# RG-LRU gate matmuls on 64-row halves of the array, both gates in one operand, and ScalarE evicting 64-partition halves

## The chip, the cores and the metric

The kernel runs on one NeuronCore of a Trainium2 chip. The metric is device time in microseconds (us) for one execution; the comparison is between medians of several runs. TensorE (PE) does the matmuls, ScalarE (ACT) the activations and most of the copies out of PSUM, VectorE (DVE) the elementwise work, GpSimd (POOL) some more of it, and SyncE (SP) issues the DMAs. Each engine runs its own instructions in program order, and semaphores order the engines against each other.

## The reference

One layer of a hybrid decoder: a pre-norm with adaLN shift and scale, one input projection split into two head groups (RG-LRU and HGRN2), one output projection, a post-norm and a residual. It is run over a prompt of 2048 tokens and over 8 decode sequences of 4 tokens. The change concerns the two gates of the RG-LRU, which are block-diagonal: 512 channels are 8 blocks of 64, and each gate multiplies a block by its own 64x64 matrix.

```python
def _rglru(x, h0, wa, ba, wx, bx, lam):
    B, L, _ = x.shape
    xb = x.reshape(B, L, N_BLK_A, BLK_A)                 # 8 blocks of 64 channels
    r = jax.nn.sigmoid(jnp.einsum('blnc,ncd->blnd', xb, wa).reshape(B, L, D_A) + ba)
    i = jax.nn.sigmoid(jnp.einsum('blnc,ncd->blnd', xb, wx).reshape(B, L, D_A) + bx)
    log_a = -C_RGLRU * jax.nn.softplus(-lam.astype(jnp.float32)) * r.astype(jnp.float32)
    a = jnp.exp(log_a)
    u = jnp.sqrt(jnp.maximum(-jnp.expm1(2.0 * log_a), 0.0)) * (i * x).astype(jnp.float32)
    u = u.at[:, 0].add(a[:, 0] * h0.astype(jnp.float32))
    _, h = lax.associative_scan(_lin_comb, (a, u), axis=1)
    return h, h[:, -1]
```

## The kernel before

The weights stay in SBUF. Projections are done as three 16-bit matmuls (`split3`, line 390) in place of one in fp32; the gates, the decayed attention of the other head group (`level`, `turn_k`, `unit`) and the transposes are fp32. A matmul in fp32 appears in the trace as two weight loads and two MATMUL records, here called passes.

The prompt goes through in 8 bodies of 256 tokens (`body(n)`; bodies 1 to 6 are one loop). The order within a body is written out by hand on each engine. On PE a body starts with the projection FR into `ring[0]`, ahead of which it waits for `i_sig` of the body before. Then come `turn_y` (transposes of the head group's rows `gbs` of the body before, which wait for `yb_ok`), the projection Q, and so on. The projections are interleaved with the levels of the attention and with the output projection of the body before (`out_rows`). The body does the head group's four heads in two halves, p = 0 and p = 1, and the 512 RG-LRU channels likewise: `gates(n, 0)` stands after `level(n, 1, 3)`, `gates(n, 1)` after `turn_k(n, 1)` and six of the eight k of the last `out_rows`. Behind `gates(n, 1)` come `unit(n, 1, 0)`, two more k of `out_rows`, `unit(n, 1, 1)`, and the next body.

In `gates(n, p)` a gate takes two matmuls (c = 0, 1), each with a 128x128 operand that holds two 64x64 blocks on its diagonal and zeros elsewhere, over 256 tokens. Gate r goes to one bank of PSUM, `aux[(1 + p) % 2]`, gate i to the other, and each has its own semaphore.

On ACT, `gates_out(n, p)` (lines 903 and 908) evicts them with a sigmoid and a bias per partition: two activations of 128x256 for r, two for i. For p = 1 the order on ACT is `k_out`, `squares_m(n-1, 2)`, `gates_out(n, 1)`, `squares_o(n, 2)` (line 872, wants the state update L1183 of DVE), `squares_m(n-1, 3)` (line 861, wants DVE's L1204), `squares_o(n, 3)`, then `decay` and `root`. The squares feed DVE's `rows(n, 1)`: twelve small steps of a Newton iteration and four products (L1195) that raise `yb_ok`, for which PE's `turn_y` waits. POOL multiplies i by its input (`gated`, L1607) and squares a (L1610).

Of the kernel before, what the change touches and what calls it, by code (L numbers as in the profile page):

```python
# [40 lines left out]
P = 128  # L41
# [3 lines left out]
CT = DA // P  # L45
# [30 lines left out]
def build(nc, x_prompt, x_sample, state_rglru_h, state_rglru_conv, state_hgrn_S, c_prompt, c_sample, ada_w, ada_b,  # L76
          pre_norm_w, post_norm_w, w_in, conv_w, conv_b, rg_wa, rg_ba, rg_wx, rg_bx, rg_lambda, hg_lb_logits,
          hg_onorm_w, w_out, y_prompt, y_sample, h_prompt, conv_prompt, S_prompt, h_sample, conv_sample, S_sample):
    with ExitStack() as ctx:
# [34 lines left out]
        wg = sb("wg", [P, 2, CT, P])  # L114
# [59 lines left out]
        gr_ps, gi_ps = Signal("gr_ps", 2), Signal("gi_ps", 2)  # L174
# [6 lines left out]
        r_sig, i_sig, a_exp, th_ok = (Signal(s, 4) for s in ("r_sig", "i_sig", "a_exp", "th_ok"))  # L181
# [110 lines left out]
        def _(sp):  # L292
# [15 lines left out]
            for i, (kind, c) in enumerate(pieces):  # L308
# [14 lines left out]
                if i == 6:  # L323
                    sp.wait_ge(zeroed, 1)
# [56 lines left out]
        def _(pe):  # L381
# [50 lines left out]
            def turn_y(n, j):  # L432

                if j == 0:
                    pe.wait_ge(yb_ok.sem, yb_ok.at(n, 8))
                    pe.wait_ge(r_sig.sem, r_sig.at(n, 4))
                else:
                    pe.wait_ge(i_sig.sem, i_sig.at(n, 4))
# [57 lines left out]
            def gates(n, p):  # L496
                pe.wait_ge(cvc.sem, cvc.at(n, 8 * p + 8))
                for w, s in ((0, gr_ps), (1, gi_ps)):
                    if p == 0 and w == 0:
                        if not isinstance(n, int) or n > 0:  # L500
                            pe.wait_ge(ytl.sem, ytl.at(n - 1, 2))
                    elif w == 1:
                        pe.wait_ge(kt_sb.sem, kt_sb.at(n, p + 1))
                    elif not (isinstance(n, int) and n == BODIES - 1):
                        pe.wait_ge(hn_lo.sem, hn_lo.at(n + 1, 2))
                    for c in range(2):
                        last = mm(aux[(1 + w + p) % 2][:, T * c:T * c + T], wg[:, w, 2 * p + c, :], xc[:, c, :],  # L507
                                  start=True, stop=True)
                    last.then_inc(s.sem, 1)
# [36 lines left out]
            def body(n, first, last_body):  # L546
# [7 lines left out]
                if not first:  # L554
                    pe.wait_ge(i_sig.sem, i_sig.at(n - 1, 4))
# [110 lines left out]
                pe.wait_ge(r_sig.sem, r_sig.at(n, 2))  # L666
                if not last_body:
                    turn_x(n + 1, 0)
                    pe.wait_ge(i_sig.sem, i_sig.at(n, 2))
# [5 lines left out]
                else:  # L675
                    pe.wait_ge(i_sig.sem, i_sig.at(n, 2))
# [45 lines left out]
            pe.wait_ge(zeroed, 3)  # L722
# [39 lines left out]
            pe.wait_ge(i_sig.sem, i_sig.at(n - 1, 4))  # L762
# [28 lines left out]
            for w in range(2):  # L791
                for c in range(CT):
                    o = TD * CT * w + TD * c
# [934 lines left out]
```

## Time and profile before

| | |
|---|---|
| median of 3 runs | 1025.9 us (1025.59 to 1026.58) |
| the profiled execution | 1026.3 us, which is its span; the page shows no other time for it |
| PE busy | 984.2 us, 96% of the span |
| DVE, ACT, POOL busy | 582.0, 430.0, 161.0 us |
| bodies 1 to 6 | a period of 108.4 us each |
| half of the RG-LRU gates in one body | 8 passes on PE, 4 activations on ACT |

A row of a timeline gives start, length, engine, line, operation, operands and how many instructions are merged in it (x8); in square brackets stands how long the engine was idle before it and what ended that. Records of PE overlap: a pass begins when the array can take it, and its record ends when its last result is out. So the step from start to start is the cost of a pass, not its length.

### The profile page before, as it was taken

How to read it: one execution, taken by the hardware profiler on the slowest of the kernel's cores; microseconds unless marked ns; L12 is line 12 of the kernel's file. 1: busy time of each engine (PE TensorE's matmuls, PEld its weight loads, DVE VectorE, ACT ScalarE, POOL GpSimd, SP SyncE). 2: the span in 40 equal slices, each digit the busy share in tenths (PEclk: the TensorE clock that was granted, in tenths of full speed). 3: DMA queues.
4: the chain of work that ended last, by engine and by line, in shares of the span. 5: the costliest groups of instructions: out<-in, count | busy, mean ns of one | idle time of the engine just before them, and what ended most of it. 6: DMA issues, size and time to landing. Idle time of an engine off the chain costs nothing.

```text
span 1026.3 us, 19994 instructions
## 1 busy us (share of the span) xinstructions
PE 984.2 (96%) x7423; PEld 714.3 (70%) x7478; DVE 582.0 (57%) x1652; ACT 430.0 (42%) x810; POOL 161.0 (16%) x208
## 2 busy tenths in 40 slices
PE   7899986899999999999999999999999999999987
PEld 3465875469775887579766976697759775887554
DVE  1453688436763576436754566366635773477445
ACT  2531747313651365135713373237413661345321
POOL 4000024301130112011110112011301130111212
PEclk9999998899999999999999999999999999999998
DMA  9984301100110011000110011001101010100413
GB/s 313 326 275 130 118 24 59 62 2 21 42 63 0 20 41 43 19 20 0 42 62 0 21 41 62 0 21 41 62 0 41 0 50 1 42 1 23 118 42 111
DMA packets 46590, 60.62 MB, mean 59 GB/s; under 512 B 2748, under 2 KB 40208, under 8 KB 46524
## 3 DMA queue, kind: packets, MB, share of 16 engines
q1 hardware_dynamic: 46524, 59.86, 17.8%
q8 instruction: 27, 0.44, 0.2%
q14 instruction: 39, 0.32, 0.1%
HBM read 48.90 MB, written 10.95 MB: 58 GB/s over the span
## 4 chain that ended last, share of the span: by engine, by line
PE 90%; DVE 5%; issue 2%; ACT 1%; DMA 1%; SPq 1%; DVEq 0%; ACTq 0%
PE ring L390 66%; PE lev L464 7%; PE aux L507 3%; PE okv L521 2%; PE lev L469 1%; PE okv L491 1%; PE lev L462 1%; PE ring L521 1%; PE okv L493 1%; PE okv L492 1%; DMA work<-in_w_in_dram 1%; PE okv L811 1%; PE aux L441 1%; PE aux L477 1%; PE aux L428 1%
## 5 line engine op out<-in xcount | busy, mean ns | idle before, releaser
L390 PE MATMUL ring<-hnh,wih 128*128 128x256 bf16 (+1 forms) x1152 | 291.1, 264 | 5.8 <-DVE hnl L1273 4.2
L390 PE MATMUL ring<-hnh,wil 128*128 128x256 bf16 (+1 forms) x1152 | 291.2, 264 | 0.0
L390 PE MATMUL ring<-hnl,wih 128*128 128x256 f16 (+1 forms) x1152 | 291.1, 264 | 0.0
L390 PE MATMUL ring<-woh,work 128*128 128x512 f16 x512 | 162.3, 379 | 1.7
L390 PEld LDWEIGHTS ring<-hnh,wih 128*128 128x128 f16 x1152 | 112.5, 100 | 18.1 <-issue 4.5
L1165 DVE TENSOR_TENSOR qq<-qq,gg 128x256 f32<-128x256 f32 x96 | 44.1, 459 | 140.1 <-PE lev L464 99.8
L390 PEld LDWEIGHTS ring<-hnl,wih 128*128 128x128 f16 x1152 | 110.6, 98 | 12.9
L390 PEld LDWEIGHTS ring<-hnh,wil 128*128 128x128 bf16 x1152 | 110.6, 98 | 12.4
L390 PE MATMUL ring<-wih,hnh 128*128 128x512 f16 (+1 forms) x264 | 101.1, 383 | 4.0 <-ACT kk L851 4.0
L390 PE MATMUL ring<-wih,hnl 128*128 128x512 f16 (+1 forms) x264 | 101.1, 383 | 1.4 <-issue 0.2
L1587 POOL TENSOR_TENSOR kk<-kk,cols 128x256 f32<-128x256 f32 x32 | 29.3, 935 | 419.3 <-ACT kk L851 419.3
L390 PE MATMUL ring<-wil,hnh 128*128 128x512 bf16 (+1 forms) x240 | 91.7, 382 | 0.0
L390 PEld LDWEIGHTS ring<-woh,work 128*128 128x128 bf16 (+1 forms) x512 | 50.2, 98 | 54.8
L464 PEld LDWEIGHTS lev<-qq,kk 128*128 128x128 f32 x640 | 80.9, 192 | 8.5 <-issue 2.3
L390 PE MATMUL ring<-wol,work 128*128 128x512 bf16 x225 | 85.3, 379 | 0.0
L464 PE MATMUL lev<-qq,kk 128*128 128x64 f32 x640 | 80.4, 268 | 1.8 <-DVE kk L1166 1.7
L1183 DVE SCALAR_TENSOR_TENSOR st<-st,gg,okv 128x128 f32<-128x128 f32 x64 | 19.4, 345 | 70.9 <-PE okv L493 70.9
L1173 DVE COPY_PREDICATED am<-lmask,lev 128x256 f32<-128x256 uint8 (+1 forms) x112 | 57.3, 511 | 0.0
L861 ACT ACTIVATE ring<-ring 128x512 f32<-128x512 f32 x32 | 18.6, 582 | 84.0 <-DVE work L1204 84.0
L1607 POOL TENSOR_TENSOR ii<-ii,xc 128x512 f32<-128x512 f32 x16 | 22.9, 1429 | 188.3 <-ACT ii L908 188.2
L390 PEld LDWEIGHTS ring<-wih,hnh 128*128 128x128 bf16 (+1 forms) x264 | 28.2, 107 | 29.6 <-ACT kk L851 4.3
L390 PEld LDWEIGHTS ring<-wih,hnl 128*128 128x128 f16 (+1 forms) x264 | 26.0, 99 | 31.8 <-issue 1.1
(310 smaller groups left out, 1585.5 us busy)
## 6 DMA issues: line engine op xcount, KB each, us to landing
xin<-in_x_prompt_dram SPq DMA_DIRECT2D x16, 512.0 KB, 3.4
work<-in_x_prompt_dram SPq DMA_DIRECT2D x16, 512.0 KB, 4.3
out_dram<-work SPq DMA_DIRECT2D x16, 512.0 KB, 2.6
work<-in_ada_w_dram SPq DMA_DIRECT2D x4, 1024.0 KB, 10.4
woh<-in_ada_w_dram SPq DMA_DIRECT2D x4, 1024.0 KB, 11.8
work<-in_w_in_dram SPq DMA_DIRECT2D x4, 1024.0 KB, 7.2
woh<-in_w_in_dram SPq DMA_DIRECT2D x4, 1024.0 KB, 8.5
wol<-in_w_in_dram SPq DMA_DIRECT2D x4, 1024.0 KB, 9.6
```

What stands on the lines that cost most here:

```text
L390: last = mm(out, a(k), b(k), start=start and k == ks[0] and j == 0, stop=stop and k == ks[-1] and j == 2)
L428: last = nc.tensor.transpose(bank[:, (k % 2) * T + P * t:(k % 2) * T + P * t + P], xin[:, t, P * k:P * k + P], ident[:, :])
L441: last = nc.tensor.transpose(aux[j][:, T * h + P * t:T * h + P * t + P], gbs[:, t, P * (2 * j + h):P * (2 * j + h) + P], ident[:, :])
L464: last = mm(lev[i % 2][:, P // 2 * hc:P // 2 * hc + P // 2], k, blocks(q, m)[:, :, 1, :], start=True, stop=True)
L507: last = mm(aux[(1 + w + p) % 2][:, T * c:T * c + T], wg[:, w, 2 * p + c, :], xc[:, c, :], start=True, stop=True)
L521: last = mm(bank[0:NS, o:o + 256], siluc[:, k, :], w[:, k, :], start=k == 0, stop=k == KT - 1)
L861: A(ring[j % 2][:, :], ring[j % 2][:, :], ACT.Square, accum_out=essq[:, j:j + 1]).then_inc(esq[j % 2].sem, 1)
L1165: V.tensor_tensor(qo, qo, g[:, :, 0:1].to_broadcast([P, nb, m]), ALU.mult).then_inc(q_upd.sem, 1)
L1173: V.copy_predicated(a[:, :, :, 1, :], msk, x).then_inc(amask.sem, 1)
L1183: V.scalar_tensor_tensor(st[:, hd, :], st[:, hd, :], gg[:, o:o + 1], okv[c][:, 2 * P + P * h:3 * P + P * h], ALU.mult, ALU.add).then_inc(s ...
L1587: G.tensor_tensor(kk[:, cols], kk[:, cols], omlb[:, hd:hd + 1].to_broadcast([P, T]), ALU.mult)\
L1607: G.tensor_tensor(ii[:, :, :], ii[:, :, :], xc[:, :, :], ALU.mult).then_inc(ix_ok.sem, 1)
```

## The change

The gate operand is no longer block-diagonal with zeros. `wg[rows, t, :]` holds for one block of 64 channels, on its 64 rows, gate r in one 64-column half and gate i in the other; on rows 64 to 127 the two halves are swapped, so that r of the even block lands on PSUM partitions 0 to 63 of `aux[0]` and r of the odd block on 64 to 127 of `aux[1]`. A matmul now contracts over 64 rows. For each c there are two of them, one on the upper and one on the lower 64 rows of the array, with one semaphore at the end of all four. ACT evicts 64 partitions at a time: four activations for r and four for i, where i is read from the other half of the partitions than it is written to. The decode gates change in the same way (8 matmuls, 16 activations). The clearing of `wg` by POOL falls away.

```diff
-        wg = sb("wg", [P, 2, CT, P])
+        wg = sb("wg", [P, CT, P])
...
                         for odd in range(2):
                             v = src[0].rearrange("(t two) c d -> two c t d", two=2)[odd]
-                            sp.dma_start(wg[64 * odd:64 * odd + 64, w, :, 64 * odd:64 * odd + 64], v).then_inc(wg_ld, 16)
+                            co = 64 * (w ^ odd)
+                            sp.dma_start(wg[64 * odd:64 * odd + 64, :, co:co + 64], v).then_inc(wg_ld, 16)
...
             def gates(n, p):
                 pe.wait_ge(cvc.sem, cvc.at(n, 8 * p + 8))
-                for w, s in ((0, gr_ps), (1, gi_ps)):
-                    if p == 0 and w == 0:
-                        if not isinstance(n, int) or n > 0:
-                            pe.wait_ge(ytl.sem, ytl.at(n - 1, 2))
-                    elif w == 1:
-                        pe.wait_ge(kt_sb.sem, kt_sb.at(n, p + 1))
-                    elif not (isinstance(n, int) and n == BODIES - 1):
-                        pe.wait_ge(hn_lo.sem, hn_lo.at(n + 1, 2))
-                    for c in range(2):
-                        last = mm(aux[(1 + w + p) % 2][:, T * c:T * c + T], wg[:, w, 2 * p + c, :], xc[:, c, :],
+                if p == 0:
+                    if not isinstance(n, int) or n > 0:
+                        pe.wait_ge(ytl.sem, ytl.at(n - 1, 2))
+                elif not (isinstance(n, int) and n == BODIES - 1):
+                    pe.wait_ge(hn_lo.sem, hn_lo.at(n + 1, 2))
+                pe.wait_ge(kt_sb.sem, kt_sb.at(n, p + 1))
+                for c in range(2):
+                    for half in range(2):
+                        rows = slice(64 * half, 64 * half + 64)
+                        last = mm(aux[half][:, T * c:T * c + T], wg[rows, 2 * p + c, :], xc[rows, c, :],
                                   start=True, stop=True)
-                    last.then_inc(s.sem, 1)
+                last.then_inc(gates_done.sem, 1)
...
-                pe.wait_ge(r_sig.sem, r_sig.at(n, 2))
+                pe.wait_ge(r_sig.sem, r_sig.at(n, 4))
+                pe.wait_ge(i_sig.sem, i_sig.at(n, 4))
                 if not last_body:
                     turn_x(n + 1, 0)
-                    pe.wait_ge(i_sig.sem, i_sig.at(n, 2))
                     turn_x(n + 1, 1)
...
             def gates_out(n, p):
 
-                act.wait_ge(gr_ps.sem, gr_ps.at(n, p + 1))
+                act.wait_ge(gates_done.sem, gates_done.at(n, p + 1))
                 act.wait_ge(iu.sem, iu.at(n, p))
                 for c in range(2):
-                    A(rr[:, c, :], aux[(1 + p) % 2][:, T * c:T * c + T], ACT.Sigmoid,
-                      bias=pcol("ba", 2 * p + c)).then_inc(r_sig.sem, 1)
-                act.wait_ge(gi_ps.sem, gi_ps.at(n, p + 1))
+                    for half in range(2):
+                        at = slice(64 * half, 64 * half + 64)
+                        A(rr[at, c, :], aux[half][at, T * c:T * c + T], ACT.Sigmoid,
+                          bias=pcol("ba", 2 * p + c)[at, :]).then_inc(r_sig.sem, 1)
                 act.wait_ge(scan.sem, scan.at(n, 2 * p))
                 for c in range(2):
-                    A(ii[:, c, :], aux[p][:, T * c:T * c + T], ACT.Sigmoid, bias=pcol("bx", 2 * p + c)).then_inc(i_sig.sem, 1)
+                    for half in range(2):
+                        at, of = slice(64 * half, 64 * half + 64), slice(64 - 64 * half, 128 - 64 * half)
+                        A(ii[at, c, :], aux[half][of, T * c:T * c + T], ACT.Sigmoid,
+                          bias=pcol("bx", 2 * p + c)[at, :]).then_inc(i_sig.sem, 1)
...
-            G.memset(wg[:, :, :, :], 0.0).then_inc(zeroed, 1)
```

On PE, in the loop of bodies 1 to 6, this is `gates(n, 1)` with what stands around it, before:

```order
L477 MATMUL aux1<-ident,kk 128x128 x3
L390 MATMUL ring1<-woh,work 128x512
L390 MATMUL ring1<-wol,work 128x512
L390 MATMUL ring1<-woh,work 128x512 x2
L390 MATMUL ring1<-wol,work 128x512
L390 MATMUL ring1<-woh,work 128x512
L497 REGISTER_ALU
L505 REGISTER_ALU [waits cvc]
L507 MATMUL aux0<-xc,wg 128x256 [waits hn_lo]
L507 MATMUL aux0<-xc,wg 128x256
L507 MATMUL aux1<-xc,wg 128x256 [waits kt_sb]
L507 MATMUL aux1<-xc,wg 128x256
```

and this is the same place in the changed kernel:

```order
L391 MATMUL ring1<-woh,work 128x512
L497 REGISTER_ALU
L502 REGISTER_ALU [waits cvc]
L507 MATMUL aux0<-xc,wg 128x256 [waits kt_sb,hn_lo]
L507 MATMUL aux1<-xc,wg 128x256
L507 MATMUL aux0<-xc,wg 128x256
L507 MATMUL aux1<-xc,wg 128x256
```

The number of matmuls is the same; the banks now alternate (the size shown is that of the output), and the wait for `kt_sb` stands ahead of the first matmul and not of the third.

On ACT, in the same loop, this is `gates_out(n, 1)` between the squares before:

```order
L861 ACTIVATE ring0,stat<-ring0 128x512 [waits mgd,e_ps]
L903 ACT_TABLE_LOAD [waits iu]
L903 ACTIVATE rr<-aux0,par 128x256 [waits gr_ps]
L903 ACTIVATE rr<-aux0,par 128x256
L908 ACTIVATE ii<-aux1,par 128x256 [waits scan,gi_ps]
L908 ACTIVATE ii<-aux1,par 128x256
L868 REGISTER_ALU
L872 ACTIVATE junk,stat<-okv0 128x128 [waits usq,s_upd]
```

and in the changed kernel:

```order
L862 ACTIVATE ring0,stat<-ring0 128x512 [waits mgd,e_ps]
L906 ACT_TABLE_LOAD [waits iu]
L906 ACTIVATE rr<-aux0,par 64x256 [waits gates_done]
L906 ACTIVATE rr<-aux1,par 64x256
L906 ACTIVATE rr<-aux0,par 64x256
L906 ACTIVATE rr<-aux1,par 64x256
L912 ACTIVATE ii<-aux0,par 64x256 [waits scan]
L912 ACTIVATE ii<-aux1,par 64x256
L912 ACTIVATE ii<-aux0,par 64x256
L912 ACTIVATE ii<-aux1,par 64x256
L869 REGISTER_ALU
L873 ACTIVATE junk,stat<-okv0 128x128 [waits usq,s_upd]
```

Four more activations stand ahead of `squares_o(n, 2)` there, with half the partitions and as many columns each.

## Rows read from the trace of the kernel before

**Rows 1.** The page: busy times by engine, and the granted clock in 40 slices.

```profile
PE 984.2 (96%) x7423; PEld 714.3 (70%) x7478; DVE 582.0 (57%) x1652; ACT 430.0 (42%) x810; POOL 161.0 (16%) x208
...
PEclk9999998899999999999999999999999999999998
```

**Rows 2.** Timeline of PE at `gates(n, 0)` and at `gates(n, 1)` of one body.

```profile
256.52 1.95 PE L507 MATMUL aux<-xc,wg 128*128 128x256 f32 x8
258.30 0.27 PE L390 MATMUL ring<-hnh,wih 128*128 128x256 bf16 x1
...
280.32 1.89 PE L507 MATMUL aux<-xc,wg 128*128 128x256 f32 x8
282.05 0.38 PE L491 MATMUL okv<-vv,am 128*128 128x128 f32 x2
```

**Rows 3.** Timeline of PE at level 7 (64 columns) and its neighbours.

```profile
272.48 0.38 PE L390 MATMUL ring<-woh,work 128*128 128x512 f16 x1
272.79 0.68 PE L469 MATMUL lev<-qq,kk 128*64 128x64 f32 x8
273.40 0.39 PE L390 MATMUL ring<-woh,work 128*128 128x512 f16 x1
```

**Rows 4.** Timeline of PE at level 6: first a window to 267.96, then the whole.

```profile
267.93 0.22 PE L469 MATMUL lev<-qq,kk 128*32 128x32 f32 x2
...
267.93 0.45 PE L469 MATMUL lev<-qq,kk 128*32 128x32 f32 x16
```

**Rows 5.** Timeline of PE in the decode part: 32-row operands, then the decode gates.

```profile
1006.61 1.15 PE L757 MATMUL lev<-vv,ktr 32*128 32x128 f32 x8
...
970.34 1.97 PE L794 MATMUL lev<-xin,wg 128*128 128x32 f32 x16
```

**Rows 6.** Timeline of ACT from `gates_out(n, 1)` on, same body as rows 2.

```profile
282.74 0.84 ACT L903 ACTIVATE rr<-aux,par 128x256 f32<-128x256 f32 x2
283.46 0.84 ACT L908 ACTIVATE ii<-aux,par 128x256 f32<-128x256 f32 x2
284.39 0.28 ACT L872 ACTIVATE junk<-okv 128x128 bf16<-128x128 f32 x1
...
285.67 0.58 ACT L861 ACTIVATE ring<-ring 128x512 f32<-128x512 f32 x1 [0.51 <-DVE work L1204]
...
286.95 0.28 ACT L872 ACTIVATE junk<-okv 128x128 bf16<-128x128 f32 x1 [0.59 <-DVE st L1183]
```

**Rows 7.** Groups of ACT, shapes apart: busy us, mean ns, idle before.

```profile
L903 ACT ACTIVATE rr<-aux,par 128x256 f32<-128x256 f32 x32 | 13.4, 471 | 30.3 <-PE aux L507 30.2
L969 ACT ACTIVATE vv<-ring 128x512 f32<-128x512 f32 x16 | 9.6, 597 | 83.0 <-PE ring L390 83.0
...
L1068 ACT ACTIVATE vv<-ring 32x512 f32<-32x512 f32 x1 | 0.6, 587 | 1.4 <-PE ring L390 1.4
```

**Rows 8.** DVE's L1195, PE's next body, and what line 441's idle waited for.

```profile
290.13 1.13 DVE L1195 SCALAR_TENSOR_TENSOR gbs<-okv,stat,gbs 128x128 f32<-128x128 f32 x4
...
286.02 0.27 PE L390 MATMUL ring<-hnh,wih 128*128 128x256 bf16 x1
...
291.31 0.44 PE L441 MATMUL aux<-ident,gbs 128*128 128x128 f32 x2
...
  DVE gbs L1195: 1.0, 6
```

**Rows 9.** Timeline of ACT around `gates_out(n, 0)`.

```profile
257.64 0.84 ACT L903 ACTIVATE rr<-aux,par 128x256 f32<-128x256 f32 x2 [3.32 <-PE aux L507]
258.50 0.84 ACT L908 ACTIVATE ii<-aux,par 128x256 f32<-128x256 f32 x2
261.25 0.60 ACT L879 ACTIVATE xa<-ring 128x512 f32<-128x512 f32 x1 [1.92 <-PE ring L390]
```

**Rows 10.** Timeline of DVE and of POOL in body 0.

```profile
147.40 3.77 DVE L1165 TENSOR_TENSOR qq<-qq,gg 128x256 f32<-128x256 f32 x1 [2.25 <-PE lev L464]
...
146.82 4.07 POOL L1627 TENSOR_TENSOR wol<-work,woh 128x2048 bf16<-128x2048 f32 x1
```

More of the change, by code:

```diff
@@ L180, in build @@
         xa_sb, ga_sil = Signal("xa_sb", 2), Signal("ga_sil", 2)
-        r_sig, i_sig, a_exp, th_ok = (Signal(s, 4) for s in ("r_sig", "i_sig", "a_exp", "th_ok"))
+        r_sig, i_sig = Signal("r_sig", 8), Signal("i_sig", 8)
+        a_exp, th_ok = Signal("a_exp", 4), Signal("th_ok", 4)
         u_sqrt = Signal("u_sqrt", 2)
@@ L435, in turn_y @@
                     pe.wait_ge(yb_ok.sem, yb_ok.at(n, 8))
-                    pe.wait_ge(r_sig.sem, r_sig.at(n, 4))
-                else:
-                    pe.wait_ge(i_sig.sem, i_sig.at(n, 4))
+                    pe.wait_ge(r_sig.sem, r_sig.at(n, 8))
+                    pe.wait_ge(i_sig.sem, i_sig.at(n, 8))
                 for h in range(2):
@@ L554, in body @@
                 if not first:
-                    pe.wait_ge(i_sig.sem, i_sig.at(n - 1, 4))
+                    pe.wait_ge(i_sig.sem, i_sig.at(n - 1, 8))
                 project(ring[0], FR, 0, n)
@@ L761, in _ @@
             pe.wait_ge(dv("hn"), 1)
-            pe.wait_ge(i_sig.sem, i_sig.at(n - 1, 4))
+            pe.wait_ge(i_sig.sem, i_sig.at(n - 1, 8))
             for i, col in enumerate([b + P * c for b in (XA, GA, Q_, FR) for c in range(CT)]):
@@ L790, in _ @@
             pe.wait_ge(dv("conv_d"), 16)
-            for w in range(2):
-                for c in range(CT):
-                    o = TD * CT * w + TD * c
-                    last = mm(lev[1][:, o:o + TD], wg[:, w, c, :], xcd[:, TD * c:TD * c + TD], start=True, stop=True)
+            pe.wait_ge(dv("gp_sb"), 1)
+            for c in range(CT):
+                for half, bank in ((0, lev[1]), (1, okv[0])):
+                    rows = slice(64 * half, 64 * half + 64)
+                    last = mm(bank[:, TD * c:TD * c + TD], wg[rows, c, :], xcd[rows, TD * c:TD * c + TD],
+                              start=True, stop=True)
             last.then_inc(dv("gates_ps"), 1)
@@ L1079, in _ @@
                 for c in range(CT):
-                    o = W4 * w + TD * c
-                    A(dst[:, TD * c:TD * c + TD], lev[1][:, o:o + TD], ACT.Sigmoid, bias=pcol(bias, c)).then_inc(dv("ri_d"), 1)
-            act.wait_ge(dv("ri_d"), 2 * CT)
+                    for half, bank in ((0, lev[1]), (1, okv[0])):
+                        at = slice(64 * half, 64 * half + 64)
+                        of = at if w == 0 else slice(64 - 64 * half, 128 - 64 * half)
+                        A(dst[at, TD * c:TD * c + TD], bank[of, TD * c:TD * c + TD], ACT.Sigmoid,
+                          bias=pcol(bias, c)[at, :]).then_inc(dv("ri_d"), 1)
+            act.wait_ge(dv("ri_d"), 4 * CT)
             for c in range(CT):
@@ L1604, in gated @@
             def gated(n, p):
-                pool.wait_ge(i_sig.sem, i_sig.at(n, 2 * p + 2))
+                pool.wait_ge(i_sig.sem, i_sig.at(n, 4 * p + 4))
                 G.tensor_tensor(ii[:, :, :], ii[:, :, :], xc[:, :, :], ALU.mult).then_inc(ix_ok.sem, 1)
```

12 lines of the change are left out of this document (5 added, 7 removed).

## The prediction

> **What bounds the kernel now.** I read the page first. PE is busy 96% of the span and every other engine under 60% [rows 1], and in bodies 1 to 6 its clock stays at the full level (the 9s of the middle slices; what lies lower are the first 200 us and the very end) [rows 1]. So in the loop PE sets the time, unless it waits. The timeline of PE shows what the gates cost it: 256.52 to 258.30, that is 1.78 us for the eight passes at p = 0, and 280.32 to 282.05, 1.73 us, at p = 1 [rows 2]. That is 0.216 us a pass. There are 16 such places, 28 us in all, and that is the most that is at stake.
>
> Then I looked for the place where PE has no slack. One exists in each body. The last of the four products L1195 ends at 290.13 + 1.13 = 291.26, and `turn_y` starts at 291.31 [rows 8]. The idle time ahead of line 441 is put down to L1195 six times, 1.0 us in all [rows 8]. So the chain of squares on ACT, Newton steps on DVE and `yb_ok` already ends together with PE's FR projection, which starts at 286.02 [rows 8]. Whatever PE gains between that chain's sources and `turn_y` is lost, and a delay on ACT in the chain goes to PE in full.
>
> **PE's side of the change.** The passes stay eight, of 256 columns each. A pass on 64 rows streams as many columns as one on 128, so one alone costs the same 0.216 us. The gain can come only from two passes at once, on different halves. The trace has no 64-row matmul in the loop. The nearest row is level 6, where matmuls of 32 columns alternate between two column parts of the array. In a window to 267.96 there are two of its passes, starting together at 267.93, and the sixteen start within 0.45 - 0.20 = 0.25 us, 0.017 us apart on average [rows 4]. At level 7, all on one part, the eight starts are (0.68 - 0.22)/7 = 0.066 us apart for twice the columns [rows 3]. Serial passes at level 6 would be some 0.033 apart; the row has half. So fp32 passes on different parts do run in pairs here. I take the same for row halves: four steps in place of eight, 4 x 0.216 = 0.86 us.
>
> Changing the shape of the array costs something. Into level 7 the step from the 512-column pass is 272.79 - 272.48 = 0.31 against 0.22 elsewhere, so 0.09; out of it the last start is at 272.79 + 0.68 - 0.22 = 273.25 and the next at 273.40, 0.15 against 0.06, so 0.09 [rows 3]. The new gates take 0.86 + 0.18 = 1.04, and with 0.05 for a first load that nothing hides (p = 0 has it already: 1.78 against 1.73 [rows 2]) 1.09 us. The gain g is 1.78 - 1.09 = 0.69 and 1.73 - 1.09 = 0.64; I take **0.65 us at each place**. Bounds: 0.86 with free switches; and -0.2, a loss, if the halves take turns, since the 32-row operands, which are all on one part, start (1.15 - 0.27)/7 = 0.126 us apart [rows 5], so that a row part alone is no faster.
> The Trainium skill ("TensorEngine Tiling (Array Packing)", Key Properties) says that changing the tiling mode drains TensorE; by the row that drain is 0.09 us each way, and it is in the sum.
>
> The new place of the wait for `kt_sb` costs nothing: on ACT `k_out` stands ahead of a square, a table load and the activations that begin at 282.74 [rows 6], and PE's gates began at 280.32 without idle time [rows 2]; both move together.
>
> **ACT's side.** The time of an activation follows the columns, not the partitions: 32x512 takes 587 ns, 128x512 597 [rows 7]. A half of 64x256 will cost what 128x256 does: 471 ns alone [rows 7], a step of 0.36 to 0.37 in a row (282.74 to 283.46 for two) [rows 6]. So `gates_out` grows by 4 x 0.36 = **1.44 us** each time.
>
> At p = 0 it is covered. r starts at 257.64 and i is over by 259.34; ACT is then idle 1.92 us until PE's projection at 261.25 [rows 9]. One semaphore for both gates lets r start where it did (the new passes are over about when the first four were: four steps of 0.216 and the switch). So ACT is free at about 260.7, and PE's projection then ends at 260.6. It is late by 0.2 at most, and behind it stand a table load and `decay`, for which nothing waits at once. So PE's 0.65 at p = 0 counts in full.
>
> At p = 1 the squares stand behind. In the old clock, ACT is through i not at 284.30 but at 285.74. The idle times that this can eat are 0.51 ahead of 285.67, 0.59 ahead of 286.95 and 0.09 ahead of 284.39 [rows 6], 1.19 together; and where two instructions stand back to back and neither waits they overlap by 0.10 (two of 0.47 in 0.84 [rows 6]), which comes three times, 0.3. That is 1.49 against 1.44: the squares end when they did, with next to nothing left. So `yb_ok` comes when it did, while PE reaches the end of the units 0.65 earlier, at 285.37, waits for `i_sig` (285.8), projects FR for 5.24 and is at `turn_y` at 291.03. There it waits 0.23 for L1195. **PE's 0.65 at p = 1 is lost in bodies 1 to 6.** Of what it had, only the 0.05 of the old lateness may come back or go; I count a body's gain as 0.65 to 0.70, times 6, is 4.0.
>
> If the halves on ACT step otherwise, this moves one to one: 0.05 us more a step makes 8 x 0.05 = 0.4 a body, 2.4 us in all.
> The Trainium skill ("ScalarE: Activation LUTs", What ACT_TABLE_LOAD costs) gives 280 ns + 0.833 ns a column for an activation with a bias pointer and an overlap of 93 ns between neighbours, so an estimate of 0.40 us a step at 256 columns. By it eight steps would take 0.3 us longer than by the row, a body would gain 0.35 to 0.4 and the time would be near 1022. The row is of the same operation, and I go by it.
>
> **The ends.** Body 0 is not bound by PE: DVE's L1165 takes 3.77 us there while POOL's L1627 runs [rows 10]. Its gates gain nothing for the end, and a later i moves POOL's work against DVE's: -0.4 to +0.5, taken as 0. In the last body p = 0 gains 0.65 and p = 1 as well, since what follows `unit` there is a long projection for the decode rows before `turn_y`: 1.3 us. The decode gates are sixteen passes in 972.14 - 970.34 = 1.80 (the length 1.97 less what the last record trails) [rows 5], one each 0.112, the pace of loading 128 columns. If loads of the two halves overlap they take 0.9 and gain 0.7 less 0.2 for the switches; if not, they lose 0.2. I take +0.3. The eight more activations there (about 1.4 us) have DVE idle time behind them. The memset at the start has nobody waiting.
>
> Sum: 4.0 + 1.3 + 0.3 = 5.6 us. The profiled execution took 1026.3, 0.4 over the median of 1025.9; from the median, 1025.9 - 5.6 = **1020.3 us**.
>
> **The rivals.**
> *Halves that overlap only in part.* The passes of one fp32 matmul share a half, and the next matmul is on the other. If passes start strictly in program order, the second pass of a matmul waits for its first, and only it overlaps with the next matmul: five steps for eight, 1.08 us, g = 0.43. Bodies gain 6 x 0.45, the last one 0.9, decode 0.2: 3.8 us, **1022.1**. Rows 4 speak against it (the first two starts coincide), but only for column parts.
> The Trainium skill ("TensorE: Matmul & The Clock Gate", Part 3) says matmuls start and end strictly in order, which is this rival's condition.
>
> *Halves that take turns (the change does not do what it says).* Eight steps and two switches: each place costs 0.2 us more. At p = 1 nothing then hides it, since the squares on ACT, now pushed to the end of their slack, and the unit that starts the chain are both later: 0.4 a body, 2.4, the last body and decode 0.6, body 0 up to 0.4: about 3.4 us, **1029.3, slower**. It decides from g = 0 down, that is when a place takes over 1.78 us. For it: there is no 64-row row in the trace. Against it: rows 4.
>
> *The ACT chain is dearer than I have it.* A 64-partition activation with a shift of partitions, or L1607 of POOL (which starts 1.4 us later and so beside the state updates), pushes the squares by another 0.4 to 0.7 a body: it takes back 2.4 to 4.2 of 5.6. The time is **1023 to 1025**. It would turn the sign only beyond 0.9 a body.
>
> **How the numbers follow.** Full overlap with the squares in time 0.50; part overlap 0.12; ACT chain dearer 0.20; turns 0.14; something else, such as a clock dip in other places, 0.04. The predicted time is the first case's. About 0.2% (2.05 us) is what a measurement of this kernel can tell from no change. Faster by more: the first two cases and half of the third, 0.71. Within: the other half of the third and some of the rest, 0.13. Slower: 0.16. The range: below, free switches (+0.2 at 8 places that count) and body 0's 0.5 give 1018.0; above, it takes in the ACT case and stops short of the turns, 1026.0. That leaves out some 0.18. The first case's own range is 1018.0 to 1021.5.
>
> **What the profile after would show.** Eight records of L507 within 1.0 us from the first to the last start, in pairs; the next instruction 1.05 to 1.1 after the first. Eight activations of 64x256 with steps of 0.36. No idle time ahead of L861 and L873 behind them. PE idle ahead of `turn_y` for 0.2 us in each loop body, by `yb_ok`, or ahead of FR, by `i_sig`. A period of 107.7. I am wrong if L507 still takes 1.7 us, or if the wait at `turn_y` is over 0.5 us.

## The result, and the profile after

The changed kernel takes 1030.63 us (median of 6 runs, 1028.62 to 1032.22) against 1027.2 for the kernel before in the same session. The ratio is 1.0037, 95% interval 1.0024 to 1.005: **slower**, by 0.4%. That is little, but the interval does not reach 1. I had forecast 1020.3 and faster. (The forecast started from 1025.9, the median of the kernel before at that time.)

The profiled execution took 1028.62 us with a span of 1026.9. Its page, with the busy times, the chain that ended last by engine, and one of the costliest groups (busy us, mean ns, idle before), answers to [rows 1]:

```profile
PE 971.8 (95%) x7423; PEld 697.9 (68%) x7478; DVE 591.2 (58%) x1652; ACT 466.3 (45%) x882; POOL 159.6 (16%) x207
...
PEclk9999997899999999999999999999999999999998
...
PE 76%; DVE 12%; ACT 6%; issue 4%; DMA 1%; SPq 1%; DVEq 0%; ACTq 0%
...
L391 PE MATMUL ring<-hnh,wih 128*128 128x256 bf16 (+1 forms) x1152 | 289.5, 262 | 13.6 <-ACT ii L912 7.2
```

TensorE has 12.4 us less to do than in [rows 1] and yet the kernel is longer: ScalarE has 36.3 us more, and the projections of line 391 wait 7.2 us for its `ii`. The clock slices are much the same as in [rows 1].

The two spans, 1026.9 here and 1026.3 in [rows 1], are not to be set against each other as the medians are. Here the time is 1.7 us over the span, and it is 1.8 in the runs `e3` and `e10`; so I estimate that the execution behind [rows 1] took 1028.0 us, near the top of its kernel's spread (1025.59 to 1028.46). The prediction took its span for its time. What follows compares periods of the loop, which repeat to 0.01 us within each of these two executions.

The timeline of PE at `gates(n, 0)` and at two successive `turn_y` shows both what TensorE gained and the period of the loop (answers to [rows 2, 8]):

```profile
291.38 0.33 PE L441 MATMUL aux<-ident,gbs 128*128 128x128 f32 x1 [0.23 <-DVE gbs L1203]
...
365.11 0.49 PE L507 MATMUL aux<-xc,wg 64*128 64x256 f32 x2
...
365.11 1.13 PE L507 MATMUL aux<-xc,wg 64*128 64x256 f32 x8
366.18 0.28 PE L391 MATMUL ring<-hnh,wih 128*128 128x256 bf16 x1
...
394.69 0.28 PE L391 MATMUL ring<-hnh,wih 128*128 128x256 bf16 x1 [1.08 <-ACT ii L912]
...
400.33 0.33 PE L441 MATMUL aux<-ident,gbs 128*128 128x128 f32 x1 [0.23 <-DVE gbs L1203]
```

The first row is a window to 365.40: two passes start together there, and the next two not before 365.43. The gates take 366.18 - 365.11 = 1.07 us where they took 1.78 [rows 2]. But the loop turns in 400.33 - 291.38 = 108.95 us, and the next turn, to 509.27, is 108.94. Before, `turn_y` stood at 291.31 [rows 8] and the next at 399.74:

```profile
399.74 0.33 PE L441 MATMUL aux<-ident,gbs 128*128 128x128 f32 x1
```

That is 108.43, with no wait. So each body is 0.51 us longer, six times 3.1 us, of the 3.4 between the medians. TensorE now waits twice a body, 1.08 us ahead of FR (for `i_sig`) and 0.23 ahead of `turn_y` (for `yb_ok`).

The timeline of ACT over `gates_out` at p = 0 and from `gates_out(n, 1)` on (one body; answers to [rows 6, 9]):

```profile
366.29 1.96 ACT L906 ACTIVATE rr<-aux,par 64x256 f32<-64x256 f32 x4 [3.48 <-PE aux L507]
368.27 1.96 ACT L912 ACTIVATE ii<-aux,par 64x256 f32<-64x256 f32 x4
...
390.62 1.95 ACT L906 ACTIVATE rr<-aux,par 64x256 f32<-64x256 f32 x4
392.60 1.95 ACT L912 ACTIVATE ii<-aux,par 64x256 f32<-64x256 f32 x4
394.58 0.28 ACT L873 ACTIVATE junk<-okv 128x128 bf16<-128x128 f32 x1
...
396.75 1.28 ACT L919 ACT_TABLE_LOAD   x1
```

Here is the loss. Four activations take 1.95 us, one of them 0.47 (the groups by line give a mean of 469 ns), so the step is (1.95 - 0.47)/3 = 0.49 us. In [rows 6] two took 0.84, a step of 0.37. From the first r to the first square it is 394.58 - 390.62 = 3.96 us where it was 284.39 - 282.74 = 1.65 [rows 6]: 2.31 us more. Both idle times behind it, 0.51 and 0.59 [rows 6], are gone, and the squares are late by what is left over. The next table load, which marks their end, is at 396.75, 6.13 us behind the first r. Before it was 5.00 us behind, by this row of ACT's timeline and 282.74 [rows 6]:

```profile
287.74 1.28 ACT L914 ACT_TABLE_LOAD   x1
```

### The profile page after: what moved, and what is told of

It reads as the page before. It is cut to its first block, busy times and chain, and to the rows that moved or that the text cites. A ratio compares the mean times of both kernels' runs of the same rounds, so it can differ in the third digit from the quotient of the medians.

```text
span 1026.9 us, 20063 instructions
## 1 busy us (share of the span) xinstructions
PE 971.8 (95%) x7423; PEld 697.9 (68%) x7478; DVE 591.2 (58%) x1652; ACT 466.3 (45%) x882; POOL 159.6 (16%) x207
## 4 chain that ended last, share of the span: by engine, by line
PE 76%; DVE 12%; ACT 6%; issue 4%; DMA 1%; SPq 1%; DVEq 0%; ACTq 0%
PE ring L391 56%; PE lev L464 6%; DVE xc L1241 2%; PE okv L521 2%; PE lev L462 1%; PE lev L469 1%; PE ring L521 1%; DVE hnl L1281 1%; ACT ii L912 1%; ACT rr L906 1%; ACT junk L873 1%; DMA work<-in_w_in_dram 1%; ACT L906 1%; DVE rr L1247 1%; DVE gbs L1203 1%
## 5 line engine op out<-in xcount | busy, mean ns | idle before, releaser
L464 PEld LDWEIGHTS lev<-qq,kk 128*128 128x128 f32 x640 | 80.9, 192 | 9.7 <-issue 3.5
L464 PE MATMUL lev<-qq,kk 128*128 128x64 f32 x640 | 80.3, 268 | 3.0 <-DVE kk L1174 3.0
L1615 POOL TENSOR_TENSOR ii<-ii,xc 128x512 f32<-128x512 f32 x16 | 20.6, 1285 | 224.7 <-ACT ii L912 224.7
L979 ACT ACTIVATE gbs<-ring 128x512 f32<-128x512 f32 x16 | 9.6, 598 | 89.7 <-PE ring L391 89.7
```

The lines of the kernel that those rows point to most:

```text
L464: last = mm(lev[i % 2][:, P // 2 * hc:P // 2 * hc + P // 2], k, blocks(q, m)[:, :, 1, :], start=True, stop=True)
L1615: G.tensor_tensor(ii[:, :, :], ii[:, :, :], xc[:, :, :], ALU.mult).then_inc(ix_ok.sem, 1)
```

## Experiments

The theory after this look was this: the period is set by the squares that stand behind `gates_out(n, 1)` on ScalarE, and they are late because a 64-partition activation does not overlap its neighbour. Three questions had to be told apart: whether it is the 64 partitions, the change of partitions or the change of bank; whether the squares or the wait at FR set the period; and whether TensorE's gain is real.

**The order of the halves** (`e1`), both stretches:

```
-for c in range(2):
-    for half in range(2):
+for half in range(2):
+    for c in range(2):
```

> The changed kernel, with ScalarE's 64-partition gate evictions in another order alone: both blocks of the lower half first, then both of the upper, so that half of the neighbours read and write the same partitions and the same bank. In the changed kernel the step from one to the next was 0.495 us, 0.36 for the 128-partition ones before. Theory A (a change of partitions or bank between neighbours costs the overlap): steps of 0.36 us inside a half, 0.49 at the changes, so the stretch of eight shrinks from 3.96 by about 4 x 0.13 = 0.5 us, the squares behind it come 0.5 earlier, and since they were 0.51 late the period of the loop falls from 108.94 us back to about 108.4; time about 1027, as the kernel before. Theory B (no 64-partition activation overlaps its neighbour): all steps 0.49, period and time as the changed kernel, about 1030.6.

It took 1026.72 us, ratio 0.9993 (0.998 to 1.0006): the whole loss was gone, though none of TensorE's gain came through. Timeline of ACT (the four together, then the second and third in windows of their own), and of PE at two `turn_y`:

```profile
390.77 1.69 ACT L906 ACTIVATE rr<-aux,par 64x256 f32<-64x256 f32 x4
...
391.14 0.46 ACT L906 ACTIVATE rr<-aux,par 64x256 f32<-64x256 f32 x1
...
391.63 0.47 ACT L906 ACTIVATE rr<-aux,par 64x256 f32<-64x256 f32 x1
...
399.94 0.33 PE L441 MATMUL aux<-ident,gbs 128*128 128x128 f32 x1 [0.23 <-DVE gbs L1203]
...
508.36 0.33 PE L441 MATMUL aux<-ident,gbs 128*128 128x128 f32 x1 [0.23 <-DVE gbs L1203]
```

From 390.77 to 391.14, inside a half, the step is 0.37, as in [rows 6]; from 391.14 to 391.63, at the change of half, it is 0.48 to 0.49. The stretch of eight is 0.5 us shorter and the period 508.36 - 399.94 = 108.42. Theory A holds, as to a change of partitions or bank: 64 partitions alone overlap as well as 128 do. TensorE still waits (0.23 us at `turn_y`), so the squares still set the period.

**The halves on ScalarE alone** (`e2`), the rest as before the change (`ii` in the same way):

```
-    A(rr[:, c, :], aux[(1 + p) % 2][:, T * c:T * c + T], ACT.Sigmoid,
-      bias=pcol("ba", 2 * p + c)).then_inc(r_sig.sem, 1)
+    for half in range(2):
+        at = slice(64 * half, 64 * half + 64)
+        A(rr[at, c, :], aux[(1 + p) % 2][at, T * c:T * c + T], ACT.Sigmoid,
+          bias=pcol("ba", 2 * p + c)[at, :]).then_inc(r_sig.sem, 1)
...
```

> The kernel before, with its PE part untouched, and ScalarE alone evicting each 128x256 gate block as two 64x256 halves, lower then upper, without a shift of partitions and both from one bank. It isolates what ScalarE's part of the change costs. Main theory (the loss of overlap does not need two banks or shifted partitions): steps of 0.49 us, the eight take 3.96 us instead of 1.55; the slack behind gates_out(n,1) is about 1.4 us, so yb_ok is about 1.0 us later a body, seven bodies, time about 1033 to 1034. Rival (it is the change of bank, or the shift, that costs): steps of 0.36, 1.44 us more a stretch, which just fits the slack, time 1027 to 1028.

1035.27 us, ratio 1.0079 (1.0058 to 1.0101). The timeline of ACT has the slow step although both halves lie in one bank and nothing is shifted:

```profile
393.19 1.95 ACT L906 ACTIVATE rr<-aux,par 64x256 f32<-64x256 f32 x4
...
402.89 0.33 PE L442 MATMUL aux<-ident,gbs 128*128 128x128 f32 x1 [0.23 <-DVE gbs L1201]
...
512.43 0.33 PE L442 MATMUL aux<-ident,gbs 128*128 128x128 f32 x1 [0.22 <-DVE gbs L1201]
```

The period is 109.54, 1.11 over 108.43. ScalarE's part of the change, alone, costs 1.1 us a body. The expected 1.0 was near. So neither a change of bank nor the shift of partitions is needed for the loss.

**TensorE's part with full-width evictions** (`e3`). Each activation takes half of r's rows and half of i's, so the gates are mixed up and the result is not the layer's; it is for the time alone:

```
-        A(rr[at, c, :], aux[half][at, T * c:T * c + T], ACT.Sigmoid,
-          bias=pcol("ba", 2 * p + c)[at, :]).then_inc(r_sig.sem, 1)
+    A(rr[:, c, :], aux[c][:, T * c:T * c + T], ACT.Sigmoid,
+      bias=pcol("ba", 2 * p + c)).then_inc(r_sig.sem, 2)
...
+    A(ii[:, c, :], aux[c][:, T - T * c:2 * T - T * c], ACT.Sigmoid,
+      bias=pcol("bx", 2 * p + c)).then_inc(i_sig.sem, 2)
```

> The changed kernel with TensorE's part as changed, but ScalarE evicting the two banks with 128-partition activations, four a stretch as before, banks alternating (each takes half of r's and half of i's rows, so that the gates are mixed up; it is for the time alone). It shows what TensorE's part is worth when ScalarE does no more than before, and whether a change of bank costs the overlap. Main theory: steps of 0.36 to 0.37 us in spite of the two banks, and the loop's period falls by 0.65 (one place a body) to 1.3 us (both): time 1018 to 1023. If a change of bank costs the overlap: steps of 0.49, 0.4 us more a stretch, which fits the slack, so nearly the same time. If TensorE's part is worth nothing: 1027.

1018.8 us, ratio 0.9928 (0.9907 to 0.9949). ACT's steps and two `turn_y` of PE:

```profile
387.92 0.84 ACT L904 ACTIVATE rr<-aux,par 128x256 f32<-128x256 f32 x2
388.65 0.84 ACT L908 ACTIVATE ii<-aux,par 128x256 f32<-128x256 f32 x2
...
395.85 0.33 PE L441 MATMUL aux<-ident,gbs 128*128 128x128 f32 x1
...
503.20 0.33 PE L441 MATMUL aux<-ident,gbs 128*128 128x128 f32 x1
```

A change of bank costs nothing (0.84 for two, over two banks). The period is 107.35, with no wait of PE: TensorE's part is worth 1.08 us a body when ScalarE does no more than before.

**FR's wait taken away** (`e4`):

```
-pe.wait_ge(i_sig.sem, i_sig.at(n - 1, 8))
+pe.wait_ge(r_sig.sem, r_sig.at(n - 1, 5))
 project(ring[0], FR, 0, n)
```

> The changed kernel with one wait changed: the FR projection of the next body, which waited for the last i half (it needs only ring[0] to have been read, which squares_m(n,2) did before), now waits for the first r half of gates_out(n,1). In the trace of the changed kernel that wait held TensorE 1.24 us a body, and after the projection it waited another 0.39 us for yb_ok. Main theory (ScalarE's queue up to the squares, then VectorE's steps to yb_ok, set the period): the 1.24 us move to the wait ahead of turn_y, which starts when it did; period 108.94, time 1030.6 +- 1. Rival (the wait at FR is what costs): period 107.7 to 108.0, time about 1022 to 1024.

1031.53 us, ratio 1.0044 (1.0031 to 1.0058). The timeline of PE:

```profile
402.27 0.33 PE L441 MATMUL aux<-ident,gbs 128*128 128x128 f32 x1 [1.47 <-DVE gbs L1203]
...
511.21 0.33 PE L441 MATMUL aux<-ident,gbs 128*128 128x128 f32 x1 [1.47 <-DVE gbs L1203]
```

The period is 108.94, as with the wait. The wait moved from FR to `turn_y`, where it is 1.47 us (1.08 and 0.23 before). So the chain to `yb_ok` sets the period, and the longest wait of the profile, the one at FR, costs nothing.

**Which side of the change of partitions** (`e7`): r lower, i upper, r upper, i lower, for each column block.

```
+    for half, dst, row, s in ((0, rr, "ba", r_sig), (1, ii, "bx", i_sig), (1, rr, "ba", r_sig), (0, ii, "bx", i_sig)):
+        at = slice(64 * half, 64 * half + 64)
+        of = at if dst is rr else slice(64 - 64 * half, 128 - 64 * half)
+        A(dst[at, c, :], aux[half][of, T * c:T * c + T], ACT.Sigmoid,
+          bias=pcol(row, 2 * p + c)[at, :]).then_inc(s.sem, 1)
```

> The changed kernel, with the four activations of a column block in the order r lower, i upper, r upper, i lower. From one to the next, in turn, only the partitions written change (r lower reads and writes 0 to 63, i upper reads 0 to 63 and writes 64 to 127), or only those read (i upper, then r upper). It tells which of the two costs the overlap, now that two banks with full width stepped at their 0.36 us or not in the run before. If a change of the partitions written costs it: steps of 0.49 and 0.37 in turn, beginning with 0.49; if a change of those read: 0.37 and 0.49 in turn; if either is enough: 0.49 throughout; if only both together: 0.37 throughout. The time is for none of these the question: about that of the changed kernel if either costs, and up to 4 us less if not.

1029.62 us, ratio 1.0028 (1.0013 to 1.0042). The timeline of ACT:

```profile
391.20 0.47 ACT L908 ACTIVATE rr<-aux,par 64x256 f32<-64x256 f32 x1
391.70 0.47 ACT L908 ACTIVATE ii<-aux,par 64x256 f32<-64x256 f32 x1
392.19 0.47 ACT L908 ACTIVATE rr<-aux,par 64x256 f32<-64x256 f32 x1
```

0.49 to 0.50 throughout. From i upper to r upper (391.70 to 392.19) only the partitions read from PSUM change, in one bank, and that is enough. From r lower to i upper (391.20 to 391.70) those written change and with them those of the bias, which is read at the same partitions, and the bank, which `e3` shows to cost nothing. That is enough as well, but this run does not tell the written side from the bias's.

**The change at p = 0 alone** (`e6`), with the halves as in `e1`; at p = 1 both functions as before:

```
 def gates(n, p):
+    if p:
+        for w, s in ((0, gr_ps), (1, gi_ps)):
...
+            for c in range(2):
+                last = mm(aux[w][:, T * c:T * c + T], wg[:, w, 2 + c, :], xc[:, c, :], start=True, stop=True)
+            last.then_inc(s.sem, 1)
+        return
...
 def gates_out(n, p):
+    if p:
...
+            A(rr[:, c, :], aux[0][:, T * c:T * c + T], ACT.Sigmoid, bias=pcol("ba", 2 + c)).then_inc(r_sig.sem, 2)
...
+            A(ii[:, c, :], aux[1][:, T * c:T * c + T], ACT.Sigmoid, bias=pcol("bx", 2 + c)).then_inc(i_sig.sem, 2)
+        return
```

> The change at one of its two places in a body alone: gates(n,0) and gates_out(n,0) as changed (both gates in one operand, two halves of the array, 64-partition evictions, the two blocks of one half as neighbours), gates(n,1) and gates_out(n,1) as before it; the decode as changed. The cost on ScalarE at p = 0 lies in a stretch where it was idle 1.92 us before and 3.48 us after. Theory: the place p = 0 gives TensorE 0.61 us a body, as it does in the run with full-width evictions (0.62 at gates(n,0), 0.46 at gates(n,1)), nothing at p = 1 waits, the period is 108.43 - 0.61 = 107.82 and the time 1022 to 1024. Rival (the 1.9 us more that ScalarE works at p = 0 are handed down its queue to gates_out(n,1), so that yb_ok is late here as well): period 108.2 or more, time 1026 or more.

1022.64 us, ratio 0.9965 (0.9955 to 0.9975): **faster than the kernel before, and so than the changed one**. Timelines of ACT at both places, and of PE:

```profile
365.27 1.69 ACT L927 ACTIVATE rr<-aux,par 64x256 f32<-64x256 f32 x4 [3.48 <-PE aux L518]
...
392.54 0.58 ACT L873 ACTIVATE ring<-ring 128x512 f32<-128x512 f32 x1 [0.52 <-DVE work L1233]
...
398.19 0.33 PE L445 MATMUL aux<-ident,gbs 128*128 128x128 f32 x1
...
506.01 0.33 PE L445 MATMUL aux<-ident,gbs 128*128 128x128 f32 x1
```

The period is 107.82, 0.61 less than before, and PE does not wait. ScalarE's idle time behind `gates_out(n, 1)` is back (0.52 against 0.51 in [rows 6]): what it does more at p = 0 is used up before it gets there.

**Both places, the squares between the i halves** (`e5`), with FR's early wait. In outline (`i_out` is the part of `gates_out` that evicts i):

```
 gates_out(n, 1)                  # the four r halves
+i_out(n, 1, ((1, 0),))           # one i half
 squares_o(n, 2); squares_m(n - 1, 3); squares_o(n, 3)
+i_out(n, 1, ((1, 1), (0, 0), (0, 1)))
```

> The changed kernel with TensorE's part whole at both places and ScalarE's halves put where they cost least: in each stretch the two blocks of one half are neighbours; in gates_out(n,1) only the four r halves and one i half stand ahead of the squares that yb_ok waits for, and the other three i halves behind them; FR waits for the first r half in place of the last i half (ring[0] is all it needs). ScalarE does as much as in the half-by-half order run (3.4 us a stretch), but about 1.3 us of it now lies behind the squares. Theory (the period was set by the squares' place in ScalarE's queue, and by nothing else of the change): squares_o(n,3) starts when VectorE's state is ready, TensorE waits for nothing, and the period is that of the run with full-width evictions, 107.36 us to 107.8; time 1019 to 1022. Rival (the 1.3 us move on: gate_out of the next body comes late, and IV waits for k_sig): period 108.4 or more, time 1027.

A miss: 1029.96 us, ratio 1.0035 (1.0023 to 1.0047), period 108.47 and 108.30 in turn. The squares were early, as planned, and `yb_ok` was not. The timelines of DVE and of POOL show why:

```profile
395.39 0.16 DVE L1142 TENSOR_TENSOR stat<-stat 128x4 f32<-128x4 f32 x1
395.59 1.27 DVE L1143 SCALAR_TENSOR_TENSOR stat<-stat 128x4 f32<-128x4 f32 x1
...
395.58 1.26 POOL L1620 TENSOR_TENSOR ii<-ii,xc 128x512 f32<-128x512 f32 x1 [15.94 <-ACT ii L914]
...
398.86 0.33 PE L441 MATMUL aux<-ident,gbs 128*128 128x128 f32 x1 [1.00 <-DVE gbs L1208]
```

A Newton step on four columns took 1.27 us, while GpSimd's product ran. [Rows 10] had the same picture in body 0 (DVE 3.77 us beside POOL 4.07). In the last body the decode's projection also waited 2.9 us, for the last i half.

**The product on GpSimd held back** (`e8`; `e9` adds the decode's early wait; `e10` holds it less long and has both), in outline:

```
 def gated(n, p):
+    if p: pool.wait_ge(a_exp.sem, a_exp.at(n, 4))              # e8, e9
+    if p: pool.wait_ge(newt_u.sem, newt_u.at(n, 2 * NEWTON))   # e10
     pool.wait_ge(i_sig.sem, i_sig.at(n, 4 * p + 4))
...
-pe.wait_ge(i_sig.sem, i_sig.at(n - 1, 8))                      # e9, e10: ahead of
+pe.wait_ge(r_sig.sem, r_sig.at(n - 1, 5))                      # the decode's projection
```

> The run with the halves split around the squares (period 108.3 to 108.47), with one wait more on GpSimd: at p = 1 the product of ii and xc waits for the exponentials too, so that it no longer starts with VectorE in the middle of the Newton steps to yb_ok. In that run one step of 0.16 us on four columns took 1.27 us, from 395.59 to 396.86, just as long as GpSimd's product over 128x512 (395.58, 1.26 us), and yb_ok came about 1.1 us late. Theory (GpSimd's product held that VectorE step, and nothing else kept the split from its gain): the step is back at 0.16 us, TensorE waits for nothing in the loop, period 107.36 to 107.5. Rival (the later product and square reach gate_out of the next body through the root): IV waits for k_sig, period 108 or more. Another rival (the long step has another cause): it stays, period 108.4.

> The same, and the decode's projection, which waited 2.94 us for the last i half of the last body in the split run, waits for the first r half, as FR does in the loop (ring[0] is all it needs). Theory: period 107.36 to 107.5, and 2 to 3 us less from the last turn of FR to the end than in the run without it: time 1018 to 1020, under the kernel with the change at one place (1022.6). Rival (the decode's end hangs on ScalarE's queue or VectorE's, not on its projection): the 2.9 us come back as a later wait, and only the loop's gain is left, 1020 to 1023.

> The split order again, with the decode's early wait, but GpSimd's product at p = 1 held only until VectorE's last Newton step (newt_u) and not until the exponentials. In the run that held it until the exponentials the step of VectorE was back at 0.16 us (399.90 and its neighbours), but the product started at 402.20, its square at 403.62 and gate_out of the next body at 407.82, 5.75 us behind turn_y, and TensorE then waited for k_sig (0.6 us a body) and for q_f (0.8). Here the product starts at about 400.9 on that scale and the square at 402.2, so the root and gate_out come 1.4 us sooner. Theory (both waits were the late root's): TensorE waits for nothing in the loop, period 107.36 to 107.5, time 1018 to 1021. Rival (1.4 us are not enough, since ScalarE's own queue has 1.3 us more ahead of gate_out than with full-width evictions): a rest of the wait for k_sig or q_f stays, period 107.6 to 108.4, time 1021 to 1026.

| run | median us | ratio to before, interval | period |
|---|---|---|---|
| `e8` | 1035.04 | 1.0094 (1.008 to 1.0107) | 109.18 |
| `e9` | 1032.46 | 1.0066 (1.0052 to 1.008) | 109.17 |
| `e10` | 1023.91 | 0.9976 (0.9966 to 0.9987) | 108.00 |

In `e8` the theory holds as far as it goes, and the first rival is what decided. The steps are all 0.16 us and `turn_y` waits no more, but GpSimd's product and square are late, and with them the root and `gate_out`. TensorE then waits 0.6 us a body for `k_sig` and 0.8 for `q_f`. Timelines of DVE, POOL, ACT and PE:

```profile
399.90 0.16 DVE L1143 SCALAR_TENSOR_TENSOR stat<-stat 128x4 f32<-128x4 f32 x1
...
402.20 1.28 POOL L1622 TENSOR_TENSOR ii<-ii,xc 128x512 f32<-128x512 f32 x1 [18.23 <-ACT aa L921]
...
405.88 0.63 ACT L927 ACTIVATE rr<-rr 128x512 f32<-128x512 f32 x1 [1.74 <-DVE rr L1254]
...
402.07 0.33 PE L441 MATMUL aux<-ident,gbs 128*128 128x128 f32 x1
...
511.25 0.33 PE L441 MATMUL aux<-ident,gbs 128*128 128x128 f32 x1
```

`e9` took 2.6 us from that, so the decode's wait was worth about the 2.9 it had in `e5`. In `e10` the product starts when the last Newton step is over, and the loop turns in 507.81 - 399.81 = 108.00. Timelines of POOL and PE:

```profile
398.76 1.27 POOL L1622 TENSOR_TENSOR ii<-ii,xc 128x512 f32<-128x512 f32 x1 [17.04 <-DVE stat L1144]
...
399.81 0.33 PE L441 MATMUL aux<-ident,gbs 128*128 128x128 f32 x1
...
507.81 0.33 PE L441 MATMUL aux<-ident,gbs 128*128 128x128 f32 x1
```

Its waits of PE from 300 to 700 us (us in all, times, longest):

```profile
PE lev L464 <- DVE qq L1162: 1.6, 4, 0.4
```

PE waits 0.4 us a body for `q_f`. Of the 0.65 us by which 108.00 stays over the 107.35 of `e3`, that is 0.4; the rest I have not traced. `e10` has the halves of the array at both places, and its period is still longer than the 107.82 of `e6`, which has them at one. The times agree with that, 1023.91 and 1022.64 us, but their ratios to the kernel before have intervals that touch.

## Why the prediction was wrong, step by step

**TensorE's side was right in kind.** Two passes start together: the pairs stand at 365.11, 365.43, 365.65 and 365.86, so there are four steps, as I had it. It is as plain in the decode gates, where the records stand apart (timeline of PE):

```profile
972.80 0.29 PE L794 MATMUL lev<-xin,wg 64*128 64x32 f32 x1
972.81 0.29 PE L794 MATMUL okv<-xin,wg 64*128 64x32 f32 x1
```

I had 1.09 us for a place with both switches in it. The trace's 1.07 at p = 0 has four steps of 0.216 and about 0.10 more in the first and in the last of them; and it leaves out the way in, which is 0.09 longer than before (from the last pass of L464, 0.20 for 0.11). The net gain is 0.61 us a body at p = 0 (`e6`: 108.43 - 107.82), where I took 0.65, and 1.08 - 0.61 = 0.47 at p = 1 (`e3`), where 0.64 was worked out. At p = 1 the timeline of PE in the changed kernel has:

```profile
388.31 1.13 PE L507 MATMUL aux<-xc,wg 64*128 64x256 f32 x8
389.37 0.49 PE L491 MATMUL okv<-vv,am 128*128 128x128 f32 x2
```

The eight passes take 1.06 us for 1.73, which is 0.67. But the step into them is 0.31 for 0.22, and the first step of L491 behind them 0.21 for 0.11. So the switches were taken too small, by little at p = 0 and by more at p = 1. Both rivals on this side, partial overlap and halves that take turns, fall. Partial overlap needed an order pass by pass. But the second matmul has its first pass at 972.81, and the first one its second pass at 972.94.
The Trainium skill ("TensorE: Matmul & The Clock Gate", Part 3) says that matmuls start and end strictly in program order. By whole matmuls this trace agrees, 972.80 and then 972.81; the prediction had carried the order over to the passes.

**The step that failed** is the one that put a half on ScalarE at "a step of 0.36 to 0.37 in a row" and so had `gates_out` grow "by 4 x 0.36 = 1.44 us each time". The duration was right, 469 ns for 471. The step was not: I took the overlap of activations on the same partitions for ones that alternate between two halves. It is 0.49 to 0.50, and from the first r to the first square it is 2.31 us more, where my sum has 1.44 less the 0.09 of idle time and the 0.10 of overlap there, that is 1.25. Behind the first square I counted 0.51 + 0.59 of idle time and two overlaps of 0.10, together 1.30. The trace gives 1.18: to the table load it is 396.75 - 394.58 = 2.17 us for 287.74 - 284.39 = 3.35. So the slack was nearly right, and the stretch was too long for it. From the first r to the table load it is 396.75 - 390.62 = 6.13 us for 287.74 - 282.74 = 5.00, that is 1.13 more, where I had 0.05 less. The start is 0.62 earlier by what p = 0 gave. The rest is the 0.51 of the period.

The sensitivity that stood beside it was right: "0.05 us more a step makes 8 x 0.05 = 0.4 a body". The step was 0.13 more, so 1.04 to 1.08 a body, and `e2` measures 1.11. The rival "the ACT chain is dearer" is what came, in kind, but I had priced it at 0.4 to 0.7 and put the point that decides at 0.9; it was beyond. The causes that I gave it, the shift of partitions and L1607 of POOL, are not needed: `e2` has no shift. I had bounded the duration from both sides and the overlap from one.
The Trainium skill ("ScalarE: Activation LUTs", What ACT_TABLE_LOAD costs) gives 280 ns + 0.833 ns a column and an overlap of 93 ns between neighbours; for 256 columns the first is an estimate of 493 ns. The trace has 469 ns for one activation, and an overlap of 0.1 us only between neighbours on the same partitions (`e1`); between others there is none, and they start 0.49 to 0.50 apart.

**The claim for p = 0** ("PE's 0.65 at p = 0 counts in full") stood: `e6` shows it for a stretch of 3.4 us. In the changed kernel, with 3.96, r at p = 1 still starts 99.24 us behind `turn_y` (390.62 - 291.38), 0.62 less than the 99.86 before (391.17 - 291.31), though at p = 0 `xa` now follows the halves without idle time. **The claim for p = 1** ("lost in bodies 1 to 6") was too mild; ScalarE's part there takes back its own place's gain and all of the other's. It is not lost by its place either: the matmuls that release the squares' sources stand behind `gates(n, 1)` on TensorE and come earlier with it, and in `e3`, where ScalarE's stretch is as short as before, its 0.47 comes through. The waits I named were the right ones, `i_sig` ahead of FR and `yb_ok` ahead of `turn_y`, but their sizes were 1.08 and 0.23 for 0.4 and 0.23, and `e4` shows that only the second is bound to the period.

**The ends.** PE's decode gates gained 1.80 - (973.82 - 972.80) = 0.78 us, where I took 0.3; on ScalarE the sixteen activations begin 0.31 apart. Timeline of PE and of ACT there:

```profile
973.82 0.39 PE L391 MATMUL ring<-woh,work 128*128 128x512 f16 x1
...
975.41 0.28 ACT L1088 ACTIVATE xin<-lev,par 64x32 f32<-64x32 f32 x1
975.72 0.28 ACT L1088 ACTIVATE xin<-okv,par 64x32 f32<-64x32 f32 x1
```

Eight stood 0.18 apart in the kernel before, by this row of its timeline ((1.54 - 0.28)/7):

```profile
972.95 1.54 ACT L1081 ACTIVATE xin<-lev,par 128x32 f32<-128x32 f32 x8
```

The last body, from its `turn_y` to the one behind the decode's projection, takes 948.06 - 836.13 = 111.93 us for 945.59 - 833.48 = 112.11. That is 0.18 less, and I had taken 1.3. The long projection for the decode rows, which I had set between p = 1 and `turn_y`, waits for the last i half itself: 0.80 us, ahead of 938.46. In `e3` the last body gives 1.1. From there to the transposes of the decode rows it is 999.10 - 948.06 = 51.04 for 997.42 - 945.59 = 51.83, so the 0.78 counts in full.

So of the 9.0 us between a gain of 5.6 and a loss of 3.4, six bodies that are each 0.51 longer and not some 0.67 shorter make 7.1, and the last body 1.1; the decode gates give back 0.5. The remaining 1.3 are not traced. They may well be the spread of the runs: the first `turn_y` of the loop stands at 291.38 in the changed kernel and at 293.33 in `e4`, which differs by one wait.

Two sums in the prediction are off by a little and decide nothing: the lower end of the range adds up to 1018.2, not 1018.0, and the chances of faster to 0.72, not 0.71.

## What to carry to other kernels

When an eviction is cut into parts, price two things, how long one part takes and how much of it overlaps its neighbour: the second is read only from neighbours that change in the same way. Write such parts so that neighbours stay on the same partitions, and cut only where the evicting engine has idle time behind it (`e6`), not in front of the chain that ends last. The longest wait of a profile need not be the one that costs: `e4` took away a wait of 1.08 us a body and got nothing.

## What the hardware showed that I had not expected

- ScalarE overlaps neighbouring activations by 0.1 us (0.47 long, 0.37 apart at 256 columns), with 64 partitions as with 128 (`e1`), and over two banks (`e3`). A change of the partitions read takes the overlap away, and so does a change of those written together with the bias's (0.48 to 0.50 apart, `e7`). At 32 columns it is 0.31 for 0.28 long.
- Two fp32 matmuls on 64-row halves of the array start 0.00 to 0.01 us apart; eight passes of 256 columns take 1.06 to 1.07 us from the first to the next instruction, where they took 1.73 to 1.78. The step into them is 0.09 longer.
- A VectorE step of 0.16 us on four columns in SBUF took 1.27 us beside GpSimd's product in SBUF, which took 1.26 from 0.01 us earlier; when that was moved away, it took 0.16 again (`e8`). VectorE's products that read PSUM and one tensor in SBUF were not held: in `e10` they take the same 1.13 us as in [rows 8], from 398.63 on, with GpSimd's product beside them from 398.76. The Trainium skill ("SBUF — State Buffer", Who interferes with whom) says that a VectorE instruction with two inputs in SBUF contends with a GpSimd instruction that reads SBUF, that one with a single input there does not, and that the order of issue decides who is blocked. This trace agrees: the step that was held is over at 396.86, 0.02 us after the product. The records do not settle the order to 0.01 us, though: in the last body of `e5` a step at 936.65, 0.01 behind the start of the product, is still 0.16 long, and the next one, at 936.84, takes 1.13.
